# Down-projection weights of the experts fetched through GpSimd instead of SP, in a two-block transformer kernel

## The reference, cut to what matters

```python
logits = (hf @ w_router) + b_router                  # 256 tokens, 32 experts
top_v, top_i = lax.top_k(logits, 4); top_w = softmax(top_v)
def expert_block(xb, e):
    gu = xb @ w_gate_up[e] + b_gate_up[e]            # 1024 x 2048 weights
    gate = minimum(gu[:, :1024], 7.0); up = clip(gu[:, 1024:], -7.0, 7.0)
    glu = gate * sigmoid(1.702 * gate)
    return ((up + 1.0) * glu) @ w_down[e] + b_down[e]  # 1024 x 1024 weights
```

## Time and profile before

| | |
|---|---|
| median of three runs | 2817.23 us (2815.74 to 2817.53) |
| the profiled execution | 2816.67 us, span 2814.7 us |
| PE busy | 2659.5 us, 94% |
| DVE, ACT busy | 51%, 35% |
| POOL busy | 0.2 us |
| HBM read | 662.81 MB, mean 236 GB/s |
| hardware DMA queue q1 | 663.89 MB, 61.3% of 16 engines |
| DMA in the MoE stage | 422 GB/s |
| mean granted clock of TensorE | 0.973 |

### The profile page before, as it was taken

How to read it: one execution, slowest core, us unless ns; L and a number is a source line. 1 busy time by engine, 2 the same in 40 slices (tenths; PEclk the granted TensorE clock), 3 DMA queues, 4 the chain that set the end, 5 groups by cost and what they waited for, 6 DMA issues and landing times.

```text
span 2814.7 us, 51094 instructions
## 1 busy us (share of the span) xinstructions
PE 2659.5 (94%) x20210; PEld 2184.1 (78%) x20210; DVE 1436.5 (51%) x2703; ACT 993.7 (35%) x1568; POOL 0.2 (0%) x4
## 2 busy tenths in 40 slices
PE   6977899999999999989899999998999999998998
PEld 6876556555555555558799988998989899987998
DVE  4554232333333233247566666666565566675765
ACT  3343112121121211235443455434433443454443
POOL 0000000000000000000000000000000000000000
PEclk9988799999999999999899999999999999998999
DMA  6334599999999999983255433554333255532452
GB/s 240 126 118 187 219 422 422 422 422 422 422 422 421 422 422 422 422 353 109 91 176 180 172 125 121 186 179 138 132 122 134 77 178 179 180 128 93 170 181 103
DMA packets 91751, 665.60 MB, mean 236 GB/s; under 512 B 10192, under 2 KB 10320, under 8 KB 11120
## 3 DMA queue, kind: packets, MB, share of 16 engines
q1 hardware_dynamic: 91632, 663.89, 61.3%
HBM read 662.81 MB, written 1.05 MB: 236 GB/s over the span
## 4 chain that ended last, share of the span: by engine, by line
PE 81%; DVE 6%; DMA 6%; ACT 3%; SPq 2%; issue 1%; DVEq 0%; ACTq 0%
PE bank L267 16%; PE bank L269 15%; PE bank L268 15%; PE bank L2523 13%; DMA big<-wdn 6%; PE bank L2540 6%; PE bank L2511 4%; DVE w_lo L257 2%; SPq L2461 2%; ACT w_hi L249 2%; PE bank L2571 2%; PE bank L2530 1%; PE bank L1344 1%; PE bank L943 1%; PE bank L963 1%
## 5 line engine op out<-in xcount | busy, mean ns | idle before, releaser
L257 DVE TENSOR_TENSOR w_lo<-ring,w_hi 128x2048 fp32r<-128x2048 f32 (+1 forms) x244 | 557.2, 2284 | 346.6 <-ACT w_hi L249 346.4
L267 PE MATMUL bank<-ht_hi,w_hi 128*128 128x256 f32 x2208 | 638.9, 289 | 9.1 <-DVE w_lo L257 7.2
L268 PE MATMUL bank<-ht_lo,w_hi 128*128 128x256 f32 x2208 | 627.4, 284 | 0.0
L269 PE MATMUL bank<-ht_hi,w_lo 128*128 128x256 f32 x2208 | 627.3, 284 | 0.0
L249 ACT ACTIVATE w_hi<-ring 128x2048 fp32r<-128x2048 f32 (+1 forms) x244 | 464.0, 1903 | 346.0 <-PE bank L269 322.5
L267 PEld LDWEIGHTS bank<-ht_hi,w_hi 128*128 128x128 f32 x2208 | 426.5, 193 | 20.2 <-DVE w_lo L257 9.3
L268 PEld LDWEIGHTS bank<-ht_lo,w_hi 128*128 128x128 f32 x2208 | 426.9, 193 | 2.7 <-issue 2.7
L269 PEld LDWEIGHTS bank<-ht_hi,w_lo 128*128 128x128 f32 x2208 | 426.3, 193 | 0.0
L2523 PE MATMUL bank<-ring,big 128*64 128x256 f32 x2048 | 237.1, 384 | 0.9 <-ACT big L2588 0.9
L2718 DVE TENSOR_SCALAR big<-bank,big 128x64 f32<-128x64 f32 x256 | 60.9, 280 | 341.4 <-PE bank L2530 341.4
L2523 PE MATMUL bank<-moe_w,big 128*64 128x256 f32 x2048 | 235.1, 382 | 0.0
(11 more groups left out here) (351 smaller groups left out, 3990.7 us busy)
## 6 DMA issues: line engine op xcount, KB each, us to landing
ring<-post SPq DMA_DIRECT2D x213, 1024.0 KB, 4.9
ring<-wgu SPq DMA_DIRECT2D x128, 1024.0 KB, 18.8
moe_w<-wgu SPq DMA_DIRECT2D x128, 1024.0 KB, 20.8
moe_w<-wdn SPq DMA_DIRECT2D x96, 1024.0 KB, 22.4
big<-wdn SPq DMA_DIRECT2D x32, 1024.0 KB, 23.7
ring<-pre SPq DMA_DIRECT2D x28, 1024.0 KB, 4.9
ring<-post SPq DMA_DIRECT2D x3, 768.0 KB, 4.2
con<-consts SPq DMA_DIRECT2D x1, 1409.5 KB, 7.8
```

Of the source, the lines that this page charges most:

```text
L257: dve.tensor_tensor(w_lo[:, u % SR, 0:w], ring[:, u % R, 0:w], f32(w_hi[:, u % SR, 0:w]), ALU.subtract).then_inc(ph.lo, 1)
L267: pe.matmul(out, wh, xh, start=start and k == k0, stop=False, **kw)
L268: pe.matmul(out, wh, xl, start=False, stop=False, **kw)
L269: mm = pe.matmul(out, wl, xh, start=False, stop=stop and k == k1 - 1, **kw)
```

## The change

The four down units of each item leave SP's queue for POOL. SP's first loads and its loop now hold only slots 0 to 7 (`KB` = 8). POOL gets a function of its own in the stage, with the first loads of slots 10, 11, 8 and 9 in this order, and a loop over the items with reloads of slots 8 to 11. Each reload waits for the same count of `moe_used` as before and steps the same `moe_in[l]`. SP's wait at the end of the stage stays.

```diff
-            for l in (10, 11, 0, 1, 2, 3, 4, 5, 6, 7, 8, 9):
+            for l in range(KB):
                 if l == 4:
                     sp.wait_ge(pre_done, N_PRE - 1)
                     sp.dma_start(bdn_s[:, :], bdown).then_inc(s_mc, 16)
                 free_at_start(sp, l)
-                src = wgu[0, l] if l < KB else wdn[0, l - KB]
-                sp.dma_start(slots[l], src).then_inc(moe_in[l], 16)
+                sp.dma_start(slots[l], wgu[0, l]).then_inc(moe_in[l], 16)
             sp.wait_ge(s_items, 1)
             n = sp.value_load(items[0:1, 0:1], min_val=E, max_val=ITEMS - 1)
             with sp.Fori(1, n) as i:
                 e = sp.value_load(items[0:1, bass.ds(i + 1 + ITEMS, 1)], min_val=0, max_val=E - 1)
-                for l in range(PER):
+                for l in range(KB):
                     sp.wait_ge(moe_used, i * PER + l + 1)
-                    src = wgu[bass.ds(e, 1), l] if l < KB else wdn[bass.ds(e, 1), l - KB]
-                    sp.dma_start(slots[l], src.rearrange("a p n -> (a p) n")).then_inc(moe_in[l], 16)
+                    sp.dma_start(slots[l], wgu[bass.ds(e, 1), l].rearrange("a p n -> (a p) n")).then_inc(moe_in[l], 16)
             sp.wait_ge(moe_used, n * PER + R)
+
+        def moe_pool(pool):
+            pool.wait_ge(pre_done, N_PRE - 4)
+            for l in (10, 11, 8, 9):
+                free_at_start(pool, l)
+                pool.dma_start(slots[l], wdn[0, l - KB]).then_inc(moe_in[l], 16)
+            pool.wait_ge(s_items, 1)
+            n = pool.value_load(items[0:1, 0:1], min_val=E, max_val=ITEMS - 1)
+            with pool.Fori(1, n) as i:
+                e = pool.value_load(items[0:1, bass.ds(i + 1 + ITEMS, 1)], min_val=0, max_val=E - 1)
+                for l in range(KB, PER):
+                    pool.wait_ge(moe_used, i * PER + l + 1)
+                    pool.dma_start(slots[l], wdn[bass.ds(e, 1), l - KB].rearrange("a p n -> (a p) n")).then_inc(moe_in[l], 16)
...
-        stage(pe=moe_pe, act=moe_act, dve=moe_dve, sp=moe_sp)
+        stage(pe=moe_pe, act=moe_act, dve=moe_dve, sp=moe_sp, pool=moe_pool)
```

More of the change, by code:

```diff
@@ L547, in program, with stage @@
         STAGES = []
-        def stage(pe=None, act=None, dve=None, sp=None):
-            STAGES.append(dict(pe=pe, act=act, dve=dve, sp=sp))
+        def stage(pe=None, act=None, dve=None, sp=None, pool=None):
+            STAGES.append(dict(pe=pe, act=act, dve=dve, sp=sp, pool=pool))
         def loads(ph, dram, u0, n, width=UW):
@@ L2797, in _ @@
                     st["act"](act)
+        @block.gpsimd
+        def _(pool):
+            for st in STAGES:
+                if st["pool"]:
+                    st["pool"](pool)
         @block.vector
```

## The result

The changed kernel takes 2822.66 us (median of 12 runs, 2819.26 to 2827.64) against 2815.56 us (12 runs, 2814.91 to 2817.79): ratio 1.0026, 95% interval 1.0018 to 1.0034, so 7 us slower. Forecast were 2824.6 us and +0.28%. The profiled execution after has a span of 2825.1 us, 10.4 more than before; it lies at the slow end of its own runs, so I read places in it, not its total.

A forecast was written before the change was run, and what follows sets the result against it. It took PE to bound the MoE stage early and DMA the last 11 experts or so. 2816.67 + 0 (first loads) + 0 (issuing) + 0 (rate) + 7.94 (order) = 2824.6 us, +0.28%; range 2811 to 2846 us.

The forecast's parts named there:

- case A: MoE stage: equal queue shares let down units overtake, G7 lands last; 2824.6 us, own range 2821 to 2829, chance 0.47.
- First loads: Before the MoE stage: all first loads are there by 278 us, PE begins at 309.07; cost and gain 0.
- Issuing: POOL's reload requests in the stage: sooner or later by an unknown amount, hidden; taken as 0, bounds 0 and 8 us.
- Rate: DMA in the stage: engines already full, a second queue changes nothing; taken as 0, bounds -8.9 and +38.5 us.
- Order: End of stage: G7 lands last instead of D3, leaving more PE work behind it; +7.94 us, bounds 0 and 21.66.
- the hand calculation for D3: Last expert: four down units at half rate take 19.9 us, so D3 lands at about 1237 to 1239 us.
- D landing last says E or C: Sign in the profile after: down units landing last means E or C, told apart by short or long PE stalls.
- E: Stage's queues served nearly in order of request, or order term offset by 0.9% more rate; 2816.7 us, chance 0.14.
- C: Down queue gets a third or less, so down units land late in every expert; +11.9, 2828.6 us, chance 0.08.
- Behind the stage: SP's next loads go out about 1234.3 us, landed by 1252.3, before the first split at 1256.6; hidden.
- B: Stage's down units move more slowly, POOL's descriptors costing engine time; 2833.9 us at 1%, at most 2863.1, chance 0.20.
- F: Two queues keep the stage's engines fuller, 433 GB/s, PE never waits; -8.9 us, 2807.8 us, chance 0.11.

The follow-up runs named there:

- e6: Kernel before, but POOL fetches all twelve units of every expert; SP requests the second block's weights after G3 of the last expert is used; ratio 1.0034.
- e2: Kernel before, but POOL fetches all twelve units in the old order; SP requests the second block's weights only after D2 of the last expert; ratio 0.9999.
- e1: Changed kernel, but for the last expert POOL requests the four down units only once G5 of that expert has landed; ratio 1.0021 to the kernel before.
- e3: Changed kernel with other units moved: POOL fetches G0 to G3, SP G4 to G7 and D0 to D3; ratio 1.0026 to the kernel before.
- e8: Kernel before with 16 slots in one ring instead of 12, SP fetching all, PE looping over four experts; ratio 1.0098.
- e5: Changed kernel, but in every expert POOL requests the down units only once G5 of that expert has landed; ratio 1.0026 to the kernel before.
- e10: Kernel before, but reloads of D3 take only half its columns, so not the full computation; ratio 0.9975.
- e4: Kernel before with a second set of four down slots, used by every other expert, SP fetching all; ratio 0.9997.
- e9: Kernel before with 16 slots in one ring, PE's first 28 experts as straight code instead of a loop over four; ratio 0.9998.
- e11: Changed kernel, but reloads of D3 take only half its columns, so not the full computation; ratio 0.9967 to the kernel before.
- e7: Changed kernel with fewer units moved: POOL fetches only D2 and D3 of every expert, SP the other ten; ratio 1.0014 to the kernel before.

## Why the prediction was right, and where it was not

The forecast time, its sign and the mechanism of case A came out. Of the 1.9 us between 2824.6 and 2822.66, 1.1 are the base, 2816.67 against 2815.56; the term itself, 7.94, stands between the 7.1 us of the medians and the 8.57 of the profile. As forecast were two queues in equal shares, an unchanged rate, waits at G7, a lag of one G unit, D0 to D2 and the transposes. The terms one by one:

- *First loads, 0.* Right: PE began at 309.81 and 309.07 us, within what the kernels above show, whose PE code up to there is one (307.68 to 309.98).
- *Issuing, 0.* Right. A load takes POOL 0.53 us of its own (SP 0.33), and POOL does nothing else. D0 of the last expert, asked for at 1218.7, landed after 9.2 us where half rate and the landing alone would be 5.0 + 2.4. The 1.8 us more are not POOL's: SP's first load beside a full queue of POOL's took 8.96 us in e6, 0.3 less. They go with the first load of a queue beside a full one, whoever issues it, and they are hidden. The bound of 8 us is ill named in the prediction: it is the time from D3's landing to D0's use. D0 itself landed 18.1 us before its use at 1246.03.
- *Rate, 0.* Right, and e2 shows it without the other terms.
- *Order, 7.94.* The lag in the profile is 8.57. Three parts make it up: the last landing is 0.58 us later, counted from the stage's first matmul (933.86 against 933.28); the work behind it is 8.09 and not 7.94, as PE resumes with G7 in 1.95 us; and PE starts 0.04 instead of 0.14 us behind the landing. 0.58 + 8.09 - 0.10 = 8.57. The share was equal: D0 to D3 of the last expert, issued at 1218.71, 1220.94, 1222.66 and 1224.38, landed after 9.2, 12.0, 15.2 and 18.4 us, that is at 1227.9, 1232.9, 1237.9 and 1242.8, 5.0 us apart, twice 2.485. The Trainium skill, "DMA: Bandwidth & Descriptors", "Queues, rings and completion order", with its round of the queues a packet at a time, agrees with this spacing.
- The step that was off is the hand calculation for D3: forecast to land at 1237 to 1239, it landed at 1242.8, 0.9 us ahead of G7. PE ended the D0 before it 1.3 us later than I had put it, the request for the next came 0.6 us behind that, and the first load in POOL's queue took the 1.8 us above. A little less share, and D3 would have been the last to land. It would still not have been the unit waited for: PE wants it at 1251.80, 9.0 us after it landed. So the sign "D landing last says E or C" was too sharp; C needs D3 some 8 us behind G7.
- *Behind the stage.* Hidden, as forecast, though the 1234.3 for SP's next load is 1.3 early by the prediction's own rows. It went out at 1236.98; the four had landed at 1253.59, and the first split began at 1257.81.
- The sentence "the stage ends at (last landing) + (PE work left behind that landing)" is true of this kernel and false as a rule. e1 and e3 end in a whole expert without a wait. What fits all of them but e8, which has stops of its own, is: each unit's landing plus all PE work from that unit on, and the latest of these sums is the end. Since PE and the engines differ by 0.76 us in 29, a lag at any unit is kept for some ten experts. In the changed kernel the lag begins where the lead of twelve units is used up for G7 and not for D3, 7.9 us of PE work earlier: POOL's interval grows first at 592 us (idle before in brackets), and PE waits in 23 experts instead of 11.

```profile
562.64 0.53 POOL L2473 DMA_DIRECT2D moe_w<-wdn  x1 [22.88 <-PE bank L2551]
...
592.25 0.53 POOL L2473 DMA_DIRECT2D moe_w<-wdn  x1 [23.42 <-PE bank L2551]
```

  23 - 11 = 12 more experts at 0.76 us are 9.1 us, the lag by another way.
- *Rivals.* B is refuted by e2. The two rules of the Trainium skill beside it did not show. A stream all from POOL keeps 422 GB/s, and first and last of its 16 steps are 1.8 us apart from beginning to end of the stage, so no engine falls behind. DVE's L2716 and L2717 (L2705, L2706 before) take the 0.25 and 0.34 us they took; in the changed kernel they meet none of POOL's issues, but in e2 they overlap them 91 times, with the same durations, and POOL's issues stay at 0.53 to 0.54 us. C did not occur, as the shares were equal; a worse order in the other direction, which is what C prices at 11.9, cost 8.07 and 7.32 us in e3 and e5. E and F did not occur; F's 8.9 us exist, as e10 shows (-8.50), but only fewer bytes gave them.

## What to carry to other kernels

When a loop streams weights with its DMA engines full, one queue in the order of use is worth more than two: a second queue brings no bandwidth and lets its units overtake, and the loss is the work of the consuming engine that lies between the unit that now comes late and the one that came last before. Whether SP or POOL issues does not matter; a second queue issued by ACT was not tried. Look for it by asking of each unit, not of the last one: when does it land, and how much work stands from there to the end.

## What the runs showed of the hardware that I had not expected

- SP's queue pushes back. An SP instruction that issues a load of 1 MiB takes 0.33 us while up to nine loads, its own included, have not landed. In the kernel before, with eleven and twelve, the medians are 1.43 and 2.15 us and the longest 3.99 (1.93 at 1213.39 us, in a row of four); it then sets SP's pace. POOL's stayed at 0.53 us in e2, with eleven on its queue too, at landings of 27.1 us.
- A PE loop body of one or two experts (e4) jumps back without a stop, a body of four stops PE for 4.6 us at each jump (e8). Straight code of 28 experts does not.
- With straight code for 28 experts (e9) half of the DMA engines fell 9 us behind the other half over the stage, at a rate only 0.6% lower. The mean rate does not show it; the steps of a load's semaphore do.
- The runs of the changed kernel spread over 8.4 us, those of before over 2.9 (2.9 to 6.6 beside the later kernels). Part of it can be seen in the profiles: L325 behind the stage takes 3.71 us in most (before, e1, e2, e4, e5, e6, e8), 5.39 in others (after, e3, e9, e10, e11) and 6.72 in e7, at granted clocks of 1.00, 0.69 and 0.55. Why is open.
